# First block's attention with its scores run three steps ahead instead of two, one PSUM bank and one slot of 512 columns per step

## The reference, cut to what matters

```python
def causal_block_attention(q_nope, q_rope, k_nope, k_rope, v):      # "mla": 8 heads, 512 keys, causal
    def one_block(args):                                            # 128 queries at a time
        qn, qr, i = args
        s = (jnp.einsum('bqhd,bkhd->bhqk', qn, k_nope)
             + jnp.einsum('bqhr,bkr->bhqk', qr, k_rope)).astype(jnp.float32) * scale
        s = jnp.where(k_idx[None, :] <= q_idx[:, None], s, NEG_INF)
        p = jax.nn.softmax(s, axis=-1).astype(v.dtype)
        return jnp.einsum('bhqk,bkhd->bqhd', p, v)

def memory_cross_attention(xq, mem_n, w_mem_kv):                    # "mem": 4 heads, 256 keys, no mask
    s = jnp.einsum('bshd,bmhd->bhsm', q, k).astype(jnp.float32) * (XATTN_HEAD_DIM ** -0.5)
    p = jax.nn.softmax(s, axis=-1).astype(v.dtype)
    return jnp.einsum('bhsm,bmhd->bshd', p, v).reshape(B, S, XATTN_DIM)
```

## Time and profile before

| | us |
|---|---|
| median of 3 runs | 3707.59 (3707.09 to 3709.43) |
| profiled execution, its own time | 3705.55 |
| profiled execution, span of its instructions | 3703.7 |
| PE busy in the span | 3548.0 (96%) |
| DVE, ACT, POOL busy | 1717.4 (46%), 1053.7 (28%), 1288.5 (35%) |
| the four mla stretches together | 77.66 |
| the two mem stretches together | 29.18 |

### The profile page before, as it was taken

One profiled execution on the slowest core, in us unless ns is written; L12 is line 12 of the kernel. 1 busy time (PEld: TensorE's weight loads), 2 busy tenths in 40 slices (PEclk: granted clock), 3 DMA queues, 4 the chain that ended last, 5 costly groups with the idle time before them and its releaser, 6 DMA issues.

```text
span 3703.7 us, 62126 instructions
## 1 busy us (share of the span) xinstructions
PE 3548.0 (96%) x23844; PEld 3004.6 (81%) x23844; DVE 1717.4 (46%) x2759; ACT 1053.7 (28%) x1590; POOL 1288.5 (35%) x568
## 2 busy tenths in 40 slices
PE   7899997999799999999999999999999999999998
PEld 5676776333599998989799999999997887778886
DVE  5545546111441466343656325642475334574246
ACT  4334222011321224333422222221224333432121
POOL 2331442233244441324034444344441323144443
PEclk9999998999899999999999999999999999999999
DMA  3211235898322231322022322222321322023232
GB/s 111 70 61 45 80 95 199 320 369 326 121 90 88 91 97 35 99 71 91 18 81 90 94 85 94 86 94 83 97 86 43 96 77 85 29 91 97 92 96 96
DMA packets 104145, 386.22 MB, mean 104 GB/s; under 512 B 23024, under 2 KB 23856, under 8 KB 91568
## 3 DMA queue, kind: packets, MB, share of 16 engines
q1 hardware_dynamic: 86048, 364.68, 29.7%
q10 hardware_dynamic: 4112, 10.83, 0.9%
q0 software_dynamic: 13824, 8.44, 0.7%
HBM read 434.19 MB, written 16.78 MB: 122 GB/s over the span
## 4 chain that ended last, share of the span: by engine, by line
PE 80%; issue 10%; DVE 4%; POOL 2%; ACT 1%; DVEq 1%; DMA 1%; POOLq 0%; SPq 0%; ACTq 0%
PE ps L650 64%; PE ps L976 4%; PE ps L769 2%; PE ps L986 2%; PE ps L787 2%; POOL w_lo L2639 2%; PE ps L756 1%; DVEq L1632 1%; PE ps L968 1%; ACT s_all L1298 1%; DVE s_all L1827 1%; PE ps L682 0%; PE ps L791 0%; DVE h_lo L2355 0%; DMA e_w_lo<-in_wexp,cs 0%
## 5 line engine op out<-in xcount | busy, mean ns | idle before, releaser
L2639 POOL TENSOR_TENSOR w_lo<-raw,w_hi 128x1024 fp32r<-128x1024 f32 (+2 forms) x466 | 1191.0, 2556 | 2145.0 <-ACT w_hi L1218 2145.0
L1218 ACT ACTIVATE w_hi<-raw 128x1024 fp32r<-128x1024 f32 (+2 forms) x466 | 511.3, 1097 | 1913.5 <-PE ps L650 1892.7
L650 PE MATMUL ps<-h_hi,w_hi 128*128 128x264 f32 (+1 forms) x4016 | 1007.0, 313 | 18.7 <-ACT aux L1235 9.1
L650 PE MATMUL ps<-h_lo,w_hi 128*128 128x264 f32 (+1 forms) x4016 | 1000.5, 311 | 0.0
L650 PE MATMUL ps<-h_hi,w_lo 128*128 128x264 f32 (+1 forms) x4016 | 998.9, 311 | 0.0
L650 PEld LDWEIGHTS ps<-h_hi,w_hi 128*128 128x128 f32 x4016 | 657.7, 189 | 70.1 <-ACT aux L1235 9.5
L650 PEld LDWEIGHTS ps<-h_hi,w_lo 128*128 128x128 f32 x4016 | 655.0, 189 | 41.4
L650 PEld LDWEIGHTS ps<-h_lo,w_hi 128*128 128x128 f32 x4016 | 654.1, 188 | 42.0 <-issue 1.4
L650 PE MATMUL ps<-hid_hi,w_hi 128*128 128x264 f32 (+2 forms) x2040 | 538.4, 319 | 12.2 <-POOL w_lo L2639 7.1
L650 PE MATMUL ps<-hid_hi,w_lo 128*128 128x264 f32 (+2 forms) x2040 | 536.2, 318 | 0.0
L650 PE MATMUL ps<-hid_lo,w_hi 128*128 128x264 f32 (+2 forms) x2040 | 533.8, 317 | 0.0
(11 more groups left out here) (368 smaller groups left out, 3448.3 us busy)
## 6 DMA issues: line engine op xcount, KB each, us to landing
raw<-in_w SPq DMA_DIRECT2D x384, 512.0 KB, 3.6
raw<-in_w SPq DMA_DIRECT2D x64, 704.0 KB, 4.1
e_hid_hi<-in_wexp SPq DMA_DIRECT2D x24, 1024.0 KB, 7.3
e_hid_lo<-in_wexp SPq DMA_DIRECT2D x24, 1024.0 KB, 9.9
merged<-in_wexp SPq DMA_DIRECT2D x16, 1024.0 KB, 6.5
e_h_lo<-in_wexp SPq DMA_DIRECT2D x16, 1024.0 KB, 8.7
e_h_hi<-in_wexp SPq DMA_DIRECT2D x16, 1024.0 KB, 7.3
aux<-in_tab ACTq DMA_DIRECT2D x16, 432.0 KB, 3.8
```

Source lines behind the costliest of these rows:

```text
L650: ins = pe.matmul(ps[:, 2 * b + bank, 0:m], u, v[:, at:at + m], start=(k == 0 and i == 0), stop=(k == last and i == 2))
L1218: act.activation(w_hi[:, slot, 0:width * P], raw[:, slot, 0:width * P], ACT.Copy).then_inc(hi_done, 1)
L2639: pool.tensor_tensor(w_lo[:, slot, cols], raw[:, slot, cols], w_hi[:, slot, cols].bitcast(F32), ALU.subtract).then_inc(lo_done, 1)
```

## The change

`AHEAD` goes from 2 to 3. S of a step now waits for the step four before it, since each step has a bank of its own: `score_bank(t)` gives the banks 0, 2, 1, 3 in turn, where the two places of two banks were used with only one bank filled. The SBUF slots of this attention are four of 512 columns (`slots`) where they were three of 640. A memset of one column that stood at column 512 of a slot now goes to an unused column of `sinks`. Other users of `s_all` keep the old cut `s_sb`. The number of instructions of each kind is the same on DVE and ACT; PE has one register instruction less in the mla loop's body.

```diff
-AHEAD = 2
+AHEAD = 3
...
-        s_sb = s_all[:, 0:(AHEAD + 1) * 5 * P].rearrange("p (a c) -> p a c", c=5 * P)
+        s_sb = s_all[:, 0:3 * 5 * P].rearrange("p (a c) -> p a c", c=5 * P)
+        slots = s_all[:, 0:(AHEAD + 1) * BANK].rearrange("p (a c) -> p a c", c=BANK)
...
+        def score_bank(t):
+
+            return ps[:, 2 * (t % 2) + t // 2 % 2, :]
...
                 def scores(t):
-                    s, b = steps[t], take(t % 2)
-                    out = acc_flat(b)
+                    s = steps[t]
+                    b, k = T.acc(t % 2)
+                    pe.wait_ge(acc_free[b], k if t < 2 else k - 1)
+                    out = score_bank(t)
...
-                        ins = pe.transpose(out[:, P * m:P * (m + 1)], s_sb[:, t % (AHEAD + 1), col:col + P], ident)
+                        ins = pe.transpose(out[:, P * m:P * (m + 1)], slots[:, t % (AHEAD + 1), col:col + P], ident)
...
-                    out = s_sb[0:s.M, at, s.lo:s.hi + (s.sink is not None)]
+                    out = slots[0:s.M, at, s.lo:s.hi]
...
-                    scores, out = acc_flat(b)[0:s.M], s_sb[0:s.M, at, :]
+                    scores, out = score_bank(t)[0:s.M], slots[0:s.M, at, :]
...
-                    ve.memset(s_sb[0:s.M, at, SEQ:SEQ + 1], 0.0)
+                    ve.memset(sinks[0:s.M, 10:11], 0.0)
```

More of the change, by code:

```diff
@@ L1256, in exps @@
                     top, total = stat[0:s.M, 0, at:at + 1], stat[0:s.M, 1, at:at + 1]
-                    out = s_sb[0:s.M, at, s.lo:s.hi + (s.sink is not None)]
+                    out = slots[0:s.M, at, s.lo:s.hi]
                     if s.mode == "plain":
-                        act.activation(out, acc_flat(b)[0:s.M, s.lo:s.hi], ACT.Exp, bias=top,
+                        act.activation(out, score_bank(t)[0:s.M, s.lo:s.hi], ACT.Exp, bias=top,
                                        scale=s.scale, accum_out=total).then_inc(acc_free[b], 1)
@@ L1792, in second @@
                     settle()
-                    out = s_sb[0:s.M, at, s.lo:s.hi]
+                    out = slots[0:s.M, at, s.lo:s.hi]
                     ve.tensor_scalar(out, out, total, None, ALU.mult).then_inc(probs_ready, 1)
```

## The result

| | before | after |
|---|---|---|
| median, us | 3711.27 (20 runs, 3705.40 to 3720.99) | 3721.36 (20 runs, 3716.49 to 3731.45) |
| ratio to before, 95% interval | | 1.0028 (1.0020 to 1.0037) |
| profiled execution, its own time and span | 3705.55, 3703.7 | 3718.22, 3716.4 |
| the four mla stretches together | 77.66 | 85.08 |
| the two mem stretches together | 29.18 | 29.90 |

The changed kernel is slower by 10.1 us by the medians, 0.28% with an interval of 0.20% to 0.37%. The three runs of before that the prediction was made from had 3707.59 as their median; the twenty, with these three among them, have 3711.27, from the same kernel.

A forecast was written before the change was run, and what follows sets the result against it. PE was taken as busy nearly throughout, its idle times in mla stretches ended by DVE's N. Terms of 5.4 (mla), 0.2 (mem) and 3.6 (clock) gave +9.2 us on 3707.59: 3716.8 us, range 3710.0 to 3721.0.

The forecast's parts named there:

- the base: Whole kernel before the change: median 3707.59 us, to which the predicted difference of +9.2 us was added.
- The beginning of an mla stretch: S0 to T1 in mla: PE's 0.97 us wait ahead of T2 becomes 1.2 ahead of T1, which starts at 6.41.
- From T1 to V3: Middle of an mla stretch: PE has work all the time, and V3 starts at 12.77 where it started at 11.19.
- the closing: V3 to T5 in mla: the chain keeps its 3.29 us without S7 as cover; T5 at 16.06, was 14.48.
- the end: T5 to an mla stretch's end: 4.71 us, was 4.87; stretch 20.77, +1.42, and +5.4 us for mla.
- Mem: The two mem stretches: S2's 0.92 us wait goes, yet each stretch takes +0.1, together +0.2 us.
- The clock: Behind the gap ahead of T5, PE's clock falls in about three of four mla stretches at 1.2 each: +3.6 us.
- The clock holds: Rival: closing uncovered, but the clock falls in at most one stretch; +5.6 to +6.8, 3713.2 to 3714.4 us; chance 0.27.
- the waits go: Rival: waits at S2 in mem and T2 in mla vanish, nothing replaces them; -6.0, 3701.6 us; chance 0.05.
- one for the other: Rival: in mla the closing is uncovered but the beginning's wait really goes; +1.0, 3708.6 us; chance 0.13.
- worse: Rival: the clock falls in all six attention stretches at full price; +15.2, 3722.8 us; chance 0.07.

The follow-up runs named there:

- S7 early: Kernel before, with only PE's S7 issued ahead of T4 instead of T5; 3720.35 us in one run, second mla stretch 21.05 us.
- changed kernel again: The changed kernel, unaltered, measured once more for comparison on one chip; median 3718.36 us in 12 runs, ratio to before 1.0016.
- closing late, three ahead: Changed kernel, S and F three ahead, with the first head's closing taken off the chain; 3704.47 us in one run, mla stretch 19.20 us.
- closing late, two ahead: Changed kernel's banks and slots with AHEAD = 2 and the first head's closing taken off the chain; ratio to before 0.9992 in 10 runs.
- S7 and F7 back: Changed kernel with S7 put back behind V3 on PE and F7 behind N5 on DVE; 3712.53 us in one run.
- gap filled: Changed kernel with five additional unread products on PE behind V3, ahead of T5; median 3717.28 us in 12 runs, ratio to before 1.0006.
- S three, F two ahead, closing late: Changed kernel with DVE's F only two steps ahead and the first head's closing off the chain; median 3698.13 us in 9 runs, ratio to before 0.9963.
- F two ahead: Changed kernel with PE's S three steps ahead but DVE's F only two; 3718.59 us in one run.
- banks and slots alone: Changed kernel's four banks and 512-column slots with AHEAD = 2 as before; 3718.65 us in one run.

## Why the prediction came out as it did

**The step that failed is the base, not the change's sign or its mechanism.** The prediction put its sum on "The profiled execution took 3705.55 with a span of 3703.7, and the median is 3707.59" and gave the range only what the mechanisms left open. It said +9.2 us; the medians say +10.1, and the ratio 1.0028 of 3711.27 is +10.4, with an interval (0.20% to 0.37%) from 7.4 to 13.7. The time itself, 3721.36, is 4.6 above the 3716.8 predicted and 0.36 above the end of the range. Of these 4.6, 3.7 are the base, the term 3707.59 of the sum, which measured 3711.27 in twenty runs; 0.9 are the difference. Three runs within 2.3 us of each other were taken for the kernel's spread, where 26 runs of the same kernel lie between 3704.93 and 3725.11, with a median of 3712.78. The range should have had some 4 us more at each end for that. Why one execution of the same kernel takes longer than another is open but for a part. A look at the span without the six stretches shows that it is mostly not the stretches (span less stretches, beside the sum of PE's waits of over 1.5 us for weights of the experts from 660 to 940 us):

| trace | rest of the span | waits for expert weights |
|---|---|---|
| before | 3596.9 | 0 |
| S7 early | 3598.6 | 0 |
| changed kernel again | 3598.2 | 1.9 |
| closing late, three ahead | 3598.2 | 4.7 |
| closing late, two ahead | 3598.4 | 2.2 |
| S7 and F7 back | 3599.2 | 2.3 |
| changed kernel | 3601.4 | 4.5 |
| gap filled | 3603.9 | 5.6 |
| S three, F two ahead, closing late | 3603.3 | 2.7 |
| F two ahead | 3604.9 | 5.9 |
| banks and slots alone | 3608.7 | 7.7 |

The trace of before that the prediction started from is the lowest of all. The waits are a part of what moves and not the whole: with them taken off, the rests still lie between 3593.5 and 3601.0. Nothing ties them to the change: they are longest in the kernel with banks and slots alone, whose mla stretches are those of before, and the changed kernel's own two traces have 4.5 and 1.9.

**The beginning of an mla stretch: right.** T0 at 4.57 (4.6 forecast), T1 at 6.41 (6.41), its wait 1.08 by the record. That F3's place makes it, T1 at 5.21 with F two ahead shows.

**From T1 to V3, the closing, the end: right.** V3 at 12.77 (12.77), T5 at 16.06 (16.06), the gap 2.23 (2.2), T6 0.91 behind T5 (0.91), T7 2.45 behind T5, the value chosen between the two bounds. A stretch without a fall took 20.76 (20.77), the first 20.83: 83.11 for four, 5.45 more than before (+5.4). S7 moved alone and S7 put back show that its place makes the gap; the closing taken off shows that the chain behind it does.

**Mem: the size right, its part of the clock missed.** Without a fall the stretches took 14.85 and 14.61 (with the gap filled), +0.11 and +0.17, so +0.28 where +0.2 was taken. But "+0.2" was meant with no fall, and the clock fell in one mem stretch of the first trace (+0.45) and in both of the second (+1.22). Whether these falls are the change's isn't shown: the gap of 1.81 ahead of T5, which the kernel before has too, was followed by a fall in neither mem stretch of its own trace, but in all four mem stretches of the kernels with the banks alone and with S7 and F7 back.

**The clock: right in kind, its terms mis-sized.** I took three falls in mla at 1.2 each, +3.6. The first trace had two there, at 0.98 and 0.99 (21.74 - 20.76, 21.82 - 20.83), 2.0 in all; the second had three, 2.8 in all, so that one fall cost 0.95 on average. With the falls in mem it is 2.4 and 4.0. That makes the attention's share of the change, against the one trace of before, 5.7 + 2.4 = 8.1 and 5.7 + 4.0 = 9.7. That the 3.6 lies between 2.4 and 4.0 is in part luck: the term was too large for mla, and falls in mem, which it left out, made up for it.

**The rivals.** "The clock holds" is out by the traces; "the waits go" and "one for the other" are out by T1 at 6.41; "worse" had the clock fall in all six stretches, and five was the most. By the time alone, 3722.8 against 3721.36, it would have looked like the best of all; the base made that so. What "the waits go" described, more banks that let waits go, came true when F and the closing were moved as well: mla 77.66 to 69.01.

## What to carry to other kernels

When one engine's work is issued earlier, look at what it used to stand beside: here 1.72 us of scores covered a chain of 3.29 us through three engines, and were spent before it began. Run-ahead pays on the engine that waits, and not as a matter of course on its feeder, where one step more ahead can put one item more in front of the result that is needed first; and a chain of closing work should be put off the path before the run-ahead is deepened. A predicted time needs the spread of the base besides the uncertainty of the difference: three runs that agree within 2.3 us said nothing of a spread of 20.

## What the runs showed of the hardware that I had not expected

A gap of the same size does not always do the same. In the changed kernel 2.23 us ahead of T5 were followed by a fall in the first and third mla stretch and not in the second and fourth, with the same instructions; the fall began 1.5 to 1.7 us behind T5 and cost 0.98 to 0.99. In the second trace it began between 0.3 us ahead of T5, still in the gap, and 2.3 behind it, and cost 0.53 to 1.33. A gap of 1.35 us also stood ahead of a fall, while one of 2.23 us later did not. Both, with the stretches behind them, in the changed kernel; first the shorter gap:

```profile
494.99:496.34 1.35, 0.00 (x0) 0.00 (x0) 1.35 (x3) 1.06 (x1) 0.27 (x2) 1.00 0.34 24
496.40:500.40 4.00, 4.00 (x11) 3.15 (x12) 3.76 (x7) 0.00 (x0) 2.14 (x1) 0.57 0.48 152
```

```profile
677.62:679.85 2.23, 0.00 (x1) 0.03 (x1) 0.00 (x0) 0.00 (x0) 0.00 (x0) 1.00 0.73 188
679.90:683.90 4.00, 4.00 (x20) 1.69 (x22) 0.00 (x0) 0.00 (x0) 0.00 (x0) 1.00 1.01 426
```

What decides between them stays open. Over the eleven traces the counts are clear all the same: of the 30 stretches with a gap of 1.81 to 2.25 us ahead of T5, 21 had a fall (in mla 11 of 16, in mem 10 of 14), and of the 36 with a gap of 0.68 or less there, or with it filled, 2 had one. Neither the filled kernel nor the last one, with the gap ahead of T5 closed, had a fall in any of six stretches; but small gaps are no guarantee: the clock also fell in the first mla stretch of the changed kernel with its closing late (gaps of 0.68 and 0.54, stretch 20.63) and in the last one with S7 and F7 back (gap of 0.51, stretch 21.15). The other surprise is the table above: waits for expert weights of 1.8 to 4.1 us each, at other places in each execution, none to three of them of over 1.5 us. They come to as much as 7.7 us in one execution, beside the 10.1 of the change.
